# A whole transformer forward on one core: plain float32 products in place of three reduced-precision ones, with a ring of 22 slots

## The reference, cut to what matters

```python
def swiglu(h, w_gu, w_down):
    g, u = jnp.split(h @ w_gu, 2, axis=-1)
    return (jax.nn.silu(g) * u) @ w_down
...
for e in range(N_EXPERTS):
    out = out + gate[..., e:e + 1] * swiglu(h, w_gu[e], w_down[e])
```

## Time and profile before

| | us |
|---|---|
| three runs | 2336.64, 2333.47, 2338.13 |
| median | 2336.64 |
| the profiled execution | 2334.9 |
| its span | 2333.0 |

### The profile page before, as it was taken

The page is one execution under the profiler, slowest core; times in us unless marked ns, Lnnn a source line. Parts: engine busy times, 40 slices in busy tenths (PEclk is TensorE's granted clock), DMA queues, the critical chain, the costliest instruction groups (busy, mean ns, idle before and its releaser), DMA issues.

```text
span 2333.0 us, 28391 instructions
## 1 busy us (share of the span) xinstructions
PE 2063.1 (88%) x10314; PEld 1723.0 (74%) x10314; DVE 1723.7 (74%) x2425; ACT 1324.4 (57%) x1957; POOL 2.0 (0%) x5
## 2 busy tenths in 40 slices
PE   2955798998899879999999999999999986987997
PEld 2945588897888667787787877787887765765775
DVE  5766657545578648898888989898988876775764
ACT  2320325344565537777777777777777764434443
POOL 0000000000000000000000000000000000000000
PEclk9975569999899979999999999999999997997998
DMA  6976435654343218999999999899989982662630
GB/s 269 329 272 213 148 111 205 213 186 152 104 150 111 84 59 314 316 360 318 359 331 339 349 327 359 319 355 322 363 315 359 348 320 84 222 210 62 209 116 19
DMA packets 154067, 560.13 MB, mean 240 GB/s; under 512 B 17216, under 2 KB 17472, under 8 KB 153792
## 3 DMA queue, kind: packets, MB, share of 16 engines
q1 hardware_dynamic: 153920, 558.22, 68.5%
HBM read 557.11 MB, written 1.05 MB: 239 GB/s over the span
## 4 chain that ended last, share of the span: by engine, by line
PE 68%; DVE 15%; ACT 7%; DMA 6%; issue 3%; SPq 0%; DVEq 0%; ACTq 0%
PE ps L508 18%; PE ps L510 17%; PE ps L509 17%; PE ps L514 12%; DVE spl L497 5%; DMA ring<-in_moe_down 4%; ACT sph L485 3%; PE ps L518 3%; DVE macc L558 3%; DMA ring<-in_mod 1%; DMA ring<-in_moe_gu 1%; ACT arena L1870 0%; ACT L625 0%; DVE arena L678 0%; ACT ps L688 0%
## 5 line engine op out<-in xcount | busy, mean ns | idle before, releaser
L497 DVE TENSOR_TENSOR spl<-ring,sph 128x1024 fp32r<-128x1024 f32 x906 | 1084.6, 1221 | 387.0 <-ACT sph L485 378.1
L485 ACT ACTIVATE sph<-ring 128x1024 fp32r<-128x1024 f32 x906 | 952.3, 1059 | 631.1 <-PE ps L510 435.9
L508 PE MATMUL ps<-sph,hH 128*128 128x512 f32 (+1 forms) x1296 | 526.3, 406 | 4.8 <-DVE hL L2369 3.0
L510 PE MATMUL ps<-sph,hL 128*128 128x512 f32 (+1 forms) x1296 | 508.7, 392 | 0.0
L509 PE MATMUL ps<-spl,hH 128*128 128x512 f32 (+1 forms) x1296 | 507.5, 392 | 0.0
L508 PE MATMUL ps<-sph,rH 128*128 128x512 f32 x664 | 278.0, 419 | 21.1 <-ACT arena L2755 6.7
L508 PEld LDWEIGHTS ps<-sph,hH 128*128 128x128 f32 x1296 | 246.5, 190 | 56.9 <-issue 9.5
L510 PEld LDWEIGHTS ps<-sph,hL 128*128 128x128 f32 x1296 | 245.7, 190 | 53.2
L509 PEld LDWEIGHTS ps<-spl,hH 128*128 128x128 f32 x1296 | 246.6, 190 | 51.0 <-issue 3.8
L509 PE MATMUL ps<-spl,rH 128*128 128x512 f32 x664 | 268.1, 404 | 0.0
L510 PE MATMUL ps<-sph,rL 128*128 128x512 f32 x664 | 268.1, 404 | 0.0
(11 more groups left out here) (290 smaller groups left out, 1682.3 us busy)
## 6 DMA issues: line engine op xcount, KB each, us to landing
ring<-in_moe_gu SPq DMA_DIRECT2D x448, 512.0 KB, 6.0
ring<-in_moe_down SPq DMA_DIRECT2D x224, 512.0 KB, 6.0
ring<-in_mod SPq DMA_DIRECT2D x144, 512.0 KB, 4.9
ring<-in_w_in SPq DMA_DIRECT2D x64, 512.0 KB, 4.9
ring<-in_dense_gu SPq DMA_DIRECT2D x44, 512.0 KB, 4.6
ring<-in_ssm_w_in SPq DMA_DIRECT2D x40, 512.0 KB, 4.3
ring<-in_dense_down SPq DMA_DIRECT2D x22, 512.0 KB, 4.6
ring<-in_hyb_w_in SPq DMA_DIRECT2D x20, 512.0 KB, 6.3
```

The costliest lines, as they stand in the source:

```text
L485: a.activation(k.high[m % SPLITS][:, 0:w], raw[:, 0:w], ACT.Copy).then_inc(k.S.half_rounded, 1)
L497: v.tensor_tensor(k.low[m % SPLITS][:, 0:w], raw[:, 0:w], k.high[m % SPLITS][:, 0:w], ALU.subtract).then_inc(*k.tick(k.S.half_split, f"hal ...
L508: pe.matmul(out, a[0], b[0], start=start, stop=False, skip_group_check=True)
L510: return pe.matmul(out, a[1], b[0], start=False, stop=stop, skip_group_check=True)
```

## The change

It removes the split everywhere. The types with a reduced part, the buffers `sph` and `spl`, both split functions, `mm3` and all second copies of activations (hL, rL) go. Each triple of matmuls becomes one `mm` on float32 operands. TensorE waits for the landing of a half itself and works on the ring's slot; the slot is free when TensorE has used it (`half_used`), no longer when VectorE has subtracted. The ring has 22 slots. The order of the stream is still made by VectorE's program, six halves ahead (`come`), which now issues no instruction for it; within the hybrid projections it doesn't ask for the output weights before the attention. The norm and the gather write their result straight to `h`; inner activations are written once, by VectorE in the dense block and by ScalarE in the experts and in Mamba; the mixes are shared out, two banks to ScalarE and two to VectorE. The small products for time steps and routing are plain too. Tokens and constants are now loaded behind the first 8 pieces, small tables behind the first 22, with a semaphore of their own. The expert overflow path takes `h` as its buffer. The diff, cut to its core:

```diff
-RING = 6
+RING = 22
...
-SPLITS = 6
+AHEAD = 6
...
+        if c == 8:
+            for dst, src_ in ((k.X[:, :, :], d["x"].rearrange("(t p) n -> p t n", p=128)), (k.cst[:, :], d["cst"])):
+                sp.dma_start(dst, src_).then_inc(S.rows_landed, 16)
         if c == RING:
...
+            for dst, src_ in ((k.small[:, :], d["small"]), (k.postok[:, :], d["pos"]), (k.dtw[:, :, :], d["dtw"])):
+                sp.dma_start(dst, src_).then_inc(S.small_landed, 16)
...
         if c >= RING:
-            sp.wait_ge(*k.when(k.stream.chunks[c - RING][2]))
+            freed = k.stream.chunks[c - RING][2]
+            if isinstance(freed, int):
+                sp.wait_ge(S.half_used, freed + 1)
+            else:
+                sp.wait_ge(*k.when(freed))
...
-def split_scalar(a, k, upto):
...
-        a.activation(k.high[m % SPLITS][:, 0:w], raw[:, 0:w], ACT.Copy).then_inc(k.S.half_rounded, 1)
...
-def split_vector(v, k, upto):
...
-        v.wait_ge(k.S.half_rounded, m + 1)
-        v.tensor_tensor(k.low[m % SPLITS][:, 0:w], raw[:, 0:w], k.high[m % SPLITS][:, 0:w], ALU.subtract).then_inc(*k.tick(k.S.half_split, f"half{m}"))
+def come(k, upto):
+
+    while k.at_half <= min(upto, len(k.stream.halves) - 1):
+        m = k.at_half
+        k.at_half += 1
+        k.stream.ask(("half", m), *k.stream.halves[m], m)
...
 def half(pe, k, m):
 
-    pe.wait_ge(k.S.half_split, m + 1)
-    w = k.stream.halves[m][1]
-    return k.high[m % SPLITS][:, 0:w], k.low[m % SPLITS][:, 0:w]
...
-def mm3(pe, out, a, b, start, stop):
-    pe.matmul(out, a[0], b[0], start=start, stop=False, skip_group_check=True)
-    pe.matmul(out, a[0], b[1], start=False, stop=False, skip_group_check=True)
-    return pe.matmul(out, a[1], b[0], start=False, stop=stop, skip_group_check=True)
+    sem, value, slot = landed(k, ("half", m))
+    pe.wait_ge(sem, value)
+    return slot[:, 0:k.stream.halves[m][1]]
...
             for part in range(4):
-                w = [x.rearrange("p (k n) -> p k n", k=2) for x in half(pe, k, k.stream.at["moe_gu", q] + part)]
+                w = half(pe, k, k.stream.at["moe_gu", q] + part).rearrange("p (k n) -> p k n", k=2)
                 for kk in range(2):
                     c = 2 * part + kk
-                    last = mm3(pe, bank[:, :], [x[:, c, :] for x in E.hg[e % 2]], [x[:, kk, :] for x in w], c == 0, c == 7)
+                    last = mm(pe, bank[:, :], E.hg[e % 2][:, c, :], w[:, kk, :], c == 0, c == 7)
```

More of the change, by code:

```diff
@@ L156 @@
     "rope_ready", "roped", "rows_out", "out_ready", "out_landed",
-)
+) + tuple(f"ring_landed{i}" for i in range(RING))
 Semaphores = namedtuple("Semaphores", SEMAPHORES)
@@ L198, in __init__ @@
         self.X = sb("X", [128, NT, D])
[L199 to L206, removed]
+        self.h = sb("h", [128, KD, T])
+        self.r = sb("r", [128, HALF])
         self.macc = sb("macc", [128, 3 * D])
@@ L304, in __init__ @@
         self.tmp = A.get(4, 512)
-        self.s = [A.get(2, T) for _ in range(2)]
+        self.s = [A.get(T) for _ in range(2)]
 class MambaSpace:
@@ L724, in row_item @@
             back_steps(pe, k, "tensor", 2)
-def item_scalar(a, k, m, live=()):
-    for q in range(4):
-        split_scalar(a, k, m + q + SPLITS)
-        if live:
-            advance(live)
 def item_vector(v, k, m, back=(1, 3), live=()):
     for q in range(4):
-        split_vector(v, k, m + q + SPLITS)
+        come(k, min(m + q + AHEAD, k.stream.first["hyb_out"] - 1))
         if live:
@@ L813, in out_product @@
     for q in range(2):
-        end = mm3(pe, k.banks[2 * t + q][:, :], [x[:, c, t * 128:(t + 1) * 128] for x in act], [x[:, q * 512:(q + 1) * 512] for x in w], first, last)
+        end = mm(pe, k.banks[2 * t + q][:, :], act[:, c, t * 128:(t + 1) * 128], w[:, q * 512:(q + 1) * 512], first, last)
     return end
@@ L911, in hybrid_tensor @@
     out_banks(pe, k, "hyb")
-    pe.wait_ge(*when("hyb.low6"))
+    for c in range(0, 8, 2):
+        pe.wait_ge(*when(f"hyb.moved{c}"))
     m = k.stream.first["hyb_out"]
@@ L973, in hybrid_vector @@
     m = k.stream.first["hyb"]
-    split_vector(v, k, SPLITS - 1)
+    come(k, AHEAD - 1)
     item_vector(v, k, m)
@@ L1017, in hybrid_vector @@
     back_until(v, k, "vector", 0, "gates")
-    ticks_vector(v, k, k.stream.first["hyb_out"], 4)
+    come(k, k.stream.first["hyb_out"] + 7 + AHEAD)
     add_vector(v, k, "hyb", k.stream.first["hyb_out"] + 8, Y.va.rearrange("p t n -> p (t n)"), ("hyb.gate.copied4",), Y.tmp)
@@ L1534, in dense_tensor @@
                 for part in range(4):
-                    hi, lo = (x.rearrange("p (k n) -> p k n", k=2) for x in half(pe, k, k.stream.at["dense_gu", j] + part))
+                    w = half(pe, k, k.stream.at["dense_gu", j] + part).rearrange("p (k n) -> p k n", k=2)
                     for q in range(2):
@@ L1617, in dense_scalar @@
                     done += 1
-    squares_scalar(a, k, "ffn", k.stream.first["ssm"])
+    squares_scalar(a, k, "ffn")
 def dense_vector(v, k):
@@ L1662, in mamba_tensor @@
     for t in range(NT):
-        pe.wait_ge(*when(f"n2.low{t}.1"))
+        for c in range(2):
+            pe.wait_ge(*when(f"n2.full{t}.{c}"))
     live = [time_tensor(pe, k, beside), gate_tensor(pe, k, "ssm", 2, beside)]
@@ L2663, in second_tensor @@
                 for t in range(NT):
-                    pe.wait_ge(*when(f"n{4 + l}.low{t}.1"))
+                    for c in range(2):
+                        pe.wait_ge(*when(f"n{4 + l}.full{t}.{c}"))
                     for q in range(4):
@@ L2725, in second_attend_tensor @@
     for c in (4 * part, 4 * part + 2):
-        bank = banks.take(pe, f"s{l}.mix{c}", f"s{l}.low{c}")
+        bank = banks.take(pe, f"s{l}.mix{c}", f"s{l}.moved{c}")
         for j in range(2):
```

320 lines of the change are left out of this document (102 added, 218 removed).

## The result

The change makes the kernel slower: 2576.6 us (median of 4 runs, 2573.6 to 2580.2) against 2337.4 (2333.5 to 2339.2) for the kernel before beside it, a ratio of 1.103 (95% interval 1.101 to 1.105). The profiled execution took 2575.0 us, span 2573.0, which is 240 us more than before. The forecast was 2607 with a range of 2530 to 2690: right in sign and size, some 30 us too high.

What follows compares the result with a forecast made beforehand. TensorE was taken to bound the experts, with memory close behind. Stage terms of -4.5 + 2 - 14 + 34 + 15 + 211 + 29 = +272 us on 2334.9 gave 2607 us, range 2530 to 2690.

Steps and rivals of the forecast that it cites:

- What bounds the kernel: Experts, 46% of the run: TensorE bounds them, only some 5 us of 130 per expert not matmul work, memory close behind.
- faster rival: Whole run: splitting and weight DMA, 14% of the chain of waits (327 us), vanish as real waits, giving 2260 us; 3%.
- The price per product: Every matmul product: plain float32 costs 0.86 us against 0.681 at 512 columns (+0.179), and +0.075 at 256 columns.
- How much is paid back: Whole run: of the full 397 us price, 125 us are absorbed or paid back, estimated stage by stage.
- Attention and output: Hybrid block's attention and output: 32 products add 5.7 us, earlier fetches give back 20; net -14 us (-28 to 0).
- 20 us credited to the deep ring: Attention stretch: the ring of 22 fetches compression weights and modulation chunks during the projections, saving 20 us.
- Hybrid projections: Hybrid block's projections: products add 14.3 us, work without splits ends earlier, -12.5; net +2 us (-6 to +14).
- half the 7 us: Modulation sum after the hybrid projections: without splits its 32 one-column records should run near half of their 7 us.
- Dense, Mamba, last layers: Net +34, +15 and +29 us: longer products add 42.2, 37.3 and 57.3, partly absorbed by norms, waits, scan and attention.
- as in Mamba: Last two layers: attention between the products absorbs 15 us of their longer products, as the scan does in Mamba.
- The added wait: TensorE's new wait on landed weights: nothing behind it could be earlier; 22 slots are 34 us of traffic at 338 GB/s.
- Four full passes: Rival for all products: each of four passes costs 0.227 us (0.12 at 256 columns), about 2730 us; 5%.

Runs made afterwards that it cites:

- one pass: The kernel before with only the upper-by-upper matmul, no VectorE subtraction, slots freed by ScalarE's copy: 1910.0 us in one run.

## Why the prediction was right, and where it was off

**What bounds the kernel: right.** TensorE bounded the experts before, as the starts of matmuls showed, and it is full after. The faster rival fell with it: the 14% of the chain (327 us) that were splits and weight DMA were for the most part no gaps of TensorE. In the experts it had 50 us of them.

**The price per product: right.** +0.179 was forecast from one scatter of four records, +0.177 measured over thousands. At 256 columns the straight line gave 0.218 a record, measured 0.2159. With 1944, 640 and 16 products (the last at the forecast's 1.4 us) the full price is 344 + 46 + 1 = 391 us against 397.

**How much is paid back: the term that was too small.** 391 - 240 = 151 us came back, 125 were forecast. By stages the forecast was 28 us too high in the experts and 17 in the dense block, Mamba and the last layers, and 11 too low in attention and output. That these partly cancel is luck. For the experts the sum took 130.0 us for one, found 5 us in it without matmul work, and let 3 of them go. It explained 3.3 of the 5 us by the wait for L2388; most of the rest was the granted clock behind it, which the rows gave as 0.99 and I passed over. Over eight experts the kernel before has 50 us beyond its matmul work, more than one fairly good expert shows, and all of it went: 1234.5 us is 8 x 154.3.

The reason given for it was wrong as well. I wrote that VectorE, nearly idle, lets nothing wait; the run with the splits kept shows that an idle VectorE isn't needed, and the run with four reduced passes that a deeper ring isn't either. With products of 0.907 us the same transfers and the same splits come in time through six slots, 270 GB/s in place of 338. And 25 to 33 of the 50 us were not tied to the change at all. The kernel before has too few slots for its short products, and gets them back with eight. Of the 44 MB in 130 us and ScalarE's 97.7 us of waits I had noted that memory is close behind, but not that it already cost time.

**Attention and output: forecast -14, got -3.** The -3 are -6.7 up to the first output product, +5.7 for the longer output products, as forecast, and -2.0 for the norm behind them. So the 20 us credited to the deep ring were mostly not there. The DMA piece of 10.02 us is gone, but not the 4.11 us of "issue", which had nothing to do with the ring. In the chain of the changed kernel:

```profile
133.44 6.97 PE ps L487 x32
140.66 2.80 PE ps L487 x6
143.46 4.12 issue
...
171.15 1.28 DVE macc L531
```

The modulation steps of 1.28 us stay on VectorE's queue and on the chain; few splits ever stood there (VectorE busy 122.5 of 186 us). From the modulation sum to the output the split kernel with ten slots takes 186.8 us, the changed one 186.3, the kernel before 193.0: some 6 us are what a deeper ring is worth.

**Hybrid projections: +3.8 for +2.** The projections end earlier, but the modulation sum did not speed up: 32 one-column records took 6.97 us before and after. Two stretches show why (before the sum, the sum):

```profile
128.60:133.40 4.80, 0.54 (x2) 0.17 (x2) 2.41 (x7) 2.35 (x7) 0.00 (x0) 0.99 0.99 396
133.40:140.40 7.00, 6.96 (x32) 6.90 (x32) 0.00 (x0) 0.00 (x0) 0.00 (x0) 0.50 1.03 417
```

TensorE stood for nearly all of 4.8 us, waiting for ScalarE's gate activations and VectorE's last modulation step, and came back at a granted clock of 0.50, 1.2 GHz. The same kind of sum inside the dense block, right behind products, takes 3.9 us (423.9 to 427.8) at a mean granted clock of 0.88, so the forecast of half the 7 us needed a TensorE that had not paused. Before, the clock was at 0.50 in both sums.

**Dense, Mamba, last layers: +31.7, +10.3, +18.7 for +34, +15, +29.** The absorption was right in kind. In the dense block some 6 of its 9 us lie in one place, the modulation sum. Before, two splits stood ahead of its last steps on VectorE, TensorE waited 3.3 us, and the sum then took 6.96 us at the lower clock:

```profile
422.10 6.96 PE L514 MATMUL ps<-cst,macc 128*128 128x1 f32 x32 [3.30 <-DVE macc L558]
```

Now TensorE goes on without a wait and the sum takes 3.9 us. With the splits kept beside plain products the block isn't longer (245.9 us), so there, too, it is the longer products that give the steps time. In Mamba 37 us of price came to 10; keeping the splits costs 9 again. In the last layers 57 came to 19; keeping them costs 18 again. So the splits on the queues were a third to a half of what was absorbed there, and the scan's and softmax's latency under longer products the rest; the second part was only inferred. I had taken too little for the last layers, where I priced attention "as in Mamba" though a split stood before its softmax steps as well.

**The added wait: right with 22 slots, and only with enough.** The forecast said that nothing behind the waits could be late, as 22 slots are 34 us of traffic. With 10 slots and six halves ahead that fails by 79 us. The change of release, from the split to the last use, thus needs its depth or a shorter lookahead; 14 slots with four ahead do.

**Four full passes:** the right count of passes, the wrong price of one. The Trainium skill ("TensorE: Matmul & The Clock Gate", "Wait — 56ns, not 53.3ns?") gives a warm matmul, one at 2.4 GHz, its columns divided by 2.4 GHz and some 2.5 ns. Two passes of 512 columns in one record would be 429.2 ns by it, as an estimate; measured 429.1, and at 256 columns 215.8 for 215.9. The trace agrees for plain float32. It does not for the reduced form: the rule makes 216 ns of 512 columns and the rows have 227.

## What to carry to other kernels

Price a changed matmul from the distance between starts in a full stretch, multiply by the count, and then ask how much idle time the bounding engine has over the whole stage rather than in one good period: longer work on it can close most of that (here 40 of 50 us by itself). Before giving up a split (or any helper step) because its engine looks loaded, try the cheap resource first: here two more landing slots, paid for with one unused pair, gained 30 us where the whole change lost 240. And when a buffer's release moves to a later reader, recount the slots left beside the lookahead, since what is asked ahead now holds its slot longer.

## What was unexpected of the hardware

- A reduced-precision matmul instruction costs more than its columns. From 256 to 512 columns the distance between starts grows from 0.12 to 0.227 us, so by a straight line 0.013 us are fixed per instruction; for a plain record it grows from 0.2159 to 0.4291, with 0.003 fixed. Three reduced instructions carry 0.04 us of it, two plain records 0.005. That is why four passes against three cost a factor of 1.26 at 512 columns and 1.20 at 256, and not 1.33. The surcharge shows at the higher clock alone: at 1.2 GHz the starts are 0.427 us apart, which is 512 columns and nothing more. Why is open; VectorE's traffic is not the cause (one pass).
- One core took 394 GB/s over 250 us with the DMA engines full, and 417 in a stretch of 7 us. The Trainium skill ("Perfetto Trace Analysis", "Roofline") gives 358 GB/s as a core's share when both cores of a pair draw, and about 120% of it as the ceiling for a core alone; 394 is 110%, below that ceiling, and 417 is 116%.
- A pause of under 5 us between two dense stretches was enough to find TensorE at 1.2 GHz for the next 7 us. A wait of 3.3 us in every expert of the kernel before was followed by 3.4 us at 1.2 GHz, so it cost about half as much again.
